# First weight chunks split beside the last output tiles, and a second segment that begins with plain weight blocks

## The reference, cut to what matters

```python
def swiglu_ffn(h, w_in, w_out):
    gate, up = jnp.split(h @ w_in, 2, axis=-1)
    return (jax.nn.silu(gate) * up) @ w_out

for li in range(DEPTH):
    x = x + 0.5 * swiglu_ffn(rmsnorm(x, norms[li, 0]), ffn_w_in[li, 0], ffn_w_out[li, 0])
    h = rmsnorm(x, norms[li, 1])
    ...                                   # conformer_conv (li = 0) or attention (li = 1) gives y
    x = x + y
    x = x + 0.5 * swiglu_ffn(rmsnorm(x, norms[li, 2]), ffn_w_in[li, 1], ffn_w_out[li, 1])
    if li == N_A_LAYERS - 1:
        shared = (rmsnorm(x, norm_kv) @ w_kv).reshape(B, T, N_GROUPS, 2, HEADS_PER_GROUP, HEAD_DIM)
return rmsnorm(x, norm_final), ...
```

## Time and profile before

| | |
|---|---|
| median of 3 runs | 2461.33 us (2458.36 to 2463.57) |
| the profiled execution | 2460.06 us, its span 2458.2 us |
| TensorE busy | 2287.1 us, 93% of the span, 17414 matmuls |
| VectorE busy | 1695.7 us, 69% |
| ScalarE, GpSimd busy | 840.1 us, 34%; 227.4 us, 9% |
| mean granted clock of TensorE | 0.976 |

### The profile page before, as it was taken

How to read it: one execution, slowest core, us unless ns; L and a number is a source line. 1 busy time by engine, 2 the same in 40 slices (tenths; PEclk the granted TensorE clock), 3 DMA queues, 4 the chain that set the end, 5 groups by cost and what they waited for, 6 DMA issues and landing times.

```text
span 2458.2 us, 41111 instructions
## 1 busy us (share of the span) xinstructions
PE 2287.1 (93%) x17414; PEld 2149.9 (87%) x17414; DVE 1695.7 (69%) x2175; ACT 840.1 (34%) x1055; POOL 227.4 (9%) x210
## 2 busy tenths in 40 slices
PE   2999999879889999999998999999999977999998
PEld 1999999877489999998777999999977767999997
DVE  6894796495789947963347974984346569956973
ACT  2442343211344423432223431442145534422431
POOL 3000001201140000011000000003001131000002
PEclk9999999999899999999999999999999988999999
DMA  3353453444334435521347542533759722323321
GB/s 110 115 169 102 128 178 96 128 122 113 76 88 147 154 93 154 160 88 53 114 123 222 171 150 84 167 113 83 205 146 280 219 69 86 92 82 92 94 75 50
DMA packets 372760, 306.61 MB, mean 125 GB/s; under 512 B 13831, under 2 KB 337423, under 8 KB 371723
## 3 DMA queue, kind: packets, MB, share of 16 engines
q1 hardware_dynamic: 367451, 237.47, 34.0%
q0 software_dynamic: 5184, 67.43, 7.9%
HBM read 285.51 MB, written 70.54 MB: 145 GB/s over the span
## 4 chain that ended last, share of the span: by engine, by line
PE 83%; DVE 10%; issue 2%; ACT 2%; SPq 1%; DMA 1%; POOL 0%; POOLq 0%; DVEq 0%
PE ps L1707 29%; PE ps L1764 13%; PE ps L1766 13%; PE ps L1765 13%; PE ps L2017 2%; PE ps L2018 2%; PE ps L2019 2%; PE ps L1899 1%; PE ps L2051 1%; DVE hlS L1248 1%; PE ps L2123 1%; PE ps L2099 1%; PE ps L2134 1%; DVE cT L1466 1%; DVE hlA L1248 1%
## 5 line engine op out<-in xcount | busy, mean ns | idle before, releaser
L942 ACT CAST hlS<-blk 128x1024 fp32r<-128x1024 f32 x176 | 183.3, 1052 | 204.7 <-PE ps L1766 172.6
L1707 PE MATMUL ps<-actH,oWB 128*128 128x288 f32 x1408 | 250.1, 296 | 0.0
L1707 PE MATMUL ps<-actH,oWA 128*128 128x288 f32 x1408 | 249.9, 296 | 0.0
L1764 PE MATMUL ps<-tE,hlS 128*128 128x288 f32 x704 | 212.2, 301 | 15.5 <-DVE hlS L1248 13.1
L1385 DVE SCALAR_TENSOR_TENSOR cs<-ps,rstd 128x576 f32<-128x576 f32 x64 | 48.5, 758 | 257.4 <-PE ps L1707 257.4
L1248 DVE TENSOR_TENSOR hlS<-blk,hlS 128x1024 fp32r<-128x1024 f32 x176 | 217.2, 1238 | 0.0
L1764 PE MATMUL ps<-tM,hlA 128*128 128x288 f32 x704 | 211.4, 300 | 0.0
L1765 PE MATMUL ps<-tE,hlS 128*128 128x288 f32 x704 | 210.3, 299 | 0.0
L1766 PE MATMUL ps<-tE,hlS 128*128 128x288 f32 x704 | 209.9, 298 | 0.0
L1707 PEld LDWEIGHTS ps<-actH,oWA 128*128 128x128 f32 x1408 | 209.2, 189 | 0.7 <-DVE cs L1310 0.2
L1707 PEld LDWEIGHTS ps<-actH,oWB 128*128 128x128 f32 x1408 | 208.8, 189 | 0.0
(11 more groups left out here) (245 smaller groups left out, 5554.6 us busy)
## 6 DMA issues: line engine op xcount, KB each, us to landing
blk<-in_ffn_w_in SPq DMA_DIRECT2D x352, 256.0 KB, 4.0
raws<-in_ffn_w_out SPq DMA_DIRECT2D x64, 704.0 KB, 4.5
out_kv_sample<-in_cache_kv_w POOLq DMA_DIRECT2D x8, 4064.0 KB, 16.2
out_kv_sample<-in_cache_kv_w POOLq DMA_DIRECT2D x8, 2016.0 KB, 8.3
wst<-in_conv_w_pw SPq DMA_DIRECT2D x24, 512.0 KB, 4.2
wst<-in_w_kv SPq DMA_DIRECT2D x24, 512.0 KB, 3.9
kc<-in_cache_kv_w SPq DMA_DIRECT2D x40, 256.0 KB, 8.1
uV<-ucat SPq DMA_DIRECT2D x80, 105.5 KB, 2.2
```

Of the source, the lines that this page charges most:

```text
L942: nc.scalar.copy(o, a).then_inc(S["f_h"], 1)
L1707: nx = nc.tensor.matmul(outs[t], a, b[:, t, :], start=start and first, stop=stop and b is xh and not first)
L1764: nc.tensor.matmul(out, wh[:, cols], TERM[what][:, p, 0], start=p == 0, stop=False)
```

## The change

- Second segments get an order of their own for the first unit's products: P1, P4, P2, P5, P6, P7, P3. TensorE waits for `px` of tile 6 before P1 and for `px` of tile 7 before P2 in place of the blocks of `xT`. ScalarE's waits name all products that use a split.
- VectorE splits SA and SB of that unit before it adds `px` of tile 7 to `xT`, not after.
- The first two chunks of pw1, kv and q are split ahead of tile 6's and tile 7's turn on ScalarE and VectorE, not after tile 7's.
- kv starts chunk by chunk as the blocks of `hH` and `hL` come; the ten small products stand behind chunk 1, the square root and the reciprocals behind the splits of chunks 2 and 3. The first column block is written out of the loop.
- pw1, kv and q wait for `px` of tile 6 before their first product.

```diff
+FIRST = (("P1", "P5", "P6", "P2", "P7", "P4", "P3"), ("P1", "P4", "P2", "P5", "P6", "P7", "P3"))
+def product_table(g):
+    order = [(x, 0) for x in FIRST[g]]
...
# ScalarE: unit_high
-                last = {"A1": "P1", "A2": "P4", "A3": "P4", "SA": "P7", "SB": "P3"}[what]
-                act.wait_ge(S["f_mm"], product_no(n, g, last, u - 1))
+                users = {"A1": ("P1",), "A2": ("P2", "P4"), "A3": ("P1", "P2", "P4"), "SA": ("P6", "P7"),
+                         "SB": ("P5", "P3")}[what]
+                act.wait_ge(S["f_mm"], max(product_no(n, g, x, u - 1) for x in users))
# ScalarE: outputs
                 if g == 1:
+                    if m >= KD - 2 and AFTER[n] != "final":
+                        c = m - (KD - 2)
+                        act.wait_ge(S["f_ready"], split_no(n, 1, "out", KD - 1))
+                        split_high(CB[AFTER[n]] + c, c, SIZE[AFTER[n]])
                     gain_high(AFTER[n], m)
-            if g == 1 and AFTER[n] != "final":
-                for c in range(2):
-                    if c == 0:
-                        act.wait_ge(S["f_ready"], split_no(n, 1, "out", KD - 1))
-                    split_high(CB[AFTER[n]] + c, c, SIZE[AFTER[n]])
# ScalarE: kv
-        std_tokens("kv")
         for n in range(6):
             for s in range(4):
+                if n == 0 and s == 2:
+                    std_tokens("kv")
# VectorE: outputs
+                if g == 1 and m >= KD - 2 and AFTER[n] != "final":
+                    c = m - (KD - 2)
+                    split_low(CB[AFTER[n]] + c, c, SIZE[AFTER[n]])
                 dve.wait_ge(S["fo_mm"], out_no(n, g, m))
...
                 out_low(n, g, m + 2)
+                if g == 0 and m == KD - 1:
+                    units_start(n, 1, ("SA", "SB"))
                 dve.wait_ge(S["px_ready"], out_no(n, g, m))
                 nc.vector.tensor_tensor(xT[:, m], xT[:, m], px[m % 2], ALU.add).then_inc(S["x_ready"], 1)
                 if g == 1:
                     gain_low(AFTER[n], m)
-                elif m >= KD - 2:
-                    units_start(n, 1, ("A1", "A2") if m == KD - 2 else ("SA", "SB"))
-            if g == 1 and AFTER[n] != "final":
-                for c in range(2):
-                    split_low(CB[AFTER[n]] + c, c, SIZE[AFTER[n]])
+                elif m == KD - 2:
+                    units_start(n, 1, ("A1", "A2"))
# VectorE: kv, the reciprocals from ahead of the loop to n == 0, s == 2
...
# TensorE: first unit of a segment
+            else:
+                pe.wait_ge(S["px_ready"], out_no(n, 0, KD - 2))
+                product("P1")
+                ready("A2", 0)
+                product("P4")
+                pe.wait_ge(S["px_ready"], out_no(n, 0, KD - 1))
+                product("P2")
+                ready("SB", 0)
+                product("P5")
+                product("P6")
+                product("P7")
+                product("P3")
# TensorE: kv
-        pe.wait_ge(S["sq_ready"], SQ["kv"])
-        square_sum_tokens()
-        for k in range(KD):
-            pe.wait_ge(S["h_ready"], HB["kv"] + k + 1)
+        pe.wait_ge(S["px_ready"], out_no(1, 1, KD - 2))
+        def kv_columns(n, first):
             for s in range(4):
                 pe.wait_ge(S["w_ready"], n * 4 + (CB["kv"] + s + 1))
+                if first:
+                    pe.wait_ge(S["h_ready"], HB["kv"] + 2 * s + 2)
...
+                if first and s == 1:
+                    pe.wait_ge(S["sq_ready"], SQ["kv"])
+                    square_sum_tokens()
+        kv_columns(0, True)
+        with pe.Fori(1, 6) as n:
+            kv_columns(n, False)
```

More of the change, by code:

```diff
@@ L99, in load_table @@
     return place
-SPLIT, PRODUCT, LOAD = split_table(), product_table(), load_table()
+SPLIT, PRODUCT, LOAD = split_table(), [product_table(g) for g in range(SEGS)], load_table()
 def a_split(u, what):
@@ L113, in product_no @@
 def product_no(n, g, what, u):
-    return (SEGS * n + g) * len(PRODUCT) + PRODUCT[what, u]
+    return (SEGS * n + g) * len(PRODUCT[g]) + PRODUCT[g][what, u]
 def unit_no(n, g, u):
@@ L786, in shift_cache @@
                 if ph in FFN:
-                    pool.wait_ge(S["f_mm"], SEGS * len(PRODUCT) * FFN[ph] + start + at_ * every)
+                    pool.wait_ge(S["f_mm"], SEGS * len(PRODUCT[0]) * FFN[ph] + start + at_ * every)
                 else:
@@ L1526, in _ @@
         feed_forward(1)
[L1529 to L1533, removed]
         for n in range(6):
@@ L1536, in _ @@
                 c = 4 * n + s + 2
+                if n == 0 and s == 2:
+                    dve.wait_ge(S["stdT_ready"], 1)
+                    me.mark(nc.vector.reciprocal(rstdT[:, 0:4], rstdT[:, 0:4]))
+                    nc.vector.reciprocal(rstdT[0:SMP, 4:5], rstdT[0:SMP, 4:5]).then_inc(S["kv_evac"], 5)
+                    me.wait()
+                    dve.wait_ge(S["kv_evac"], 5)
                 if s == 3:
@@ L1731, in body @@
             def body(i, first):
+                if first:
+                    pe.wait_ge(S["px_ready"], out_no(2, 1, KD - 2))
                 for s in range(4):
@@ L1772, in ready @@
                 pe.wait_ge(S["f_ready"], split_no(n, g, what, u))
-            terms = n if g == 0 else None
             ph = f"ffn{n}_in"
-            now = KD * XV[f"ffn{n}" if g else ph]
             ready("A1", 0)
[L1778 to L1787, removed]
-            if g == 0:
+            if g == 0:
+                product("P1", n)
+                pe.wait_ge(S["x_ready"], KD * XV[ph] + KD)
+                if n == 2:
+                    pe.wait_ge(S["kv_evac"], 35)
+                ready("SB", 0)
+                product("P5", n)
+                product("P6", n)
+                product("P2", n)
                 pe.wait_ge(S["sq_ready"], SQ[ph])
                 square_sum().then_inc(S["ss_done"], 1)
-            product("P7", terms)
-            if g == 0:
+                product("P7", n)
                 pe.wait_ge(S["std_ready"], ROUND[ph])
-            product("P4", terms)
-            product("P3", terms)
+                product("P4", n)
+                product("P3", n)
+            else:
[5 more added lines that the diff above has]
+                product("P2")
+                ready("SB", 0)
+                product("P5")
+                product("P6")
+                product("P7")
+                product("P3")
             def cycle(i, u):
@@ L1924, in _ @@
         for c in range(16):
+            if c == 0:
+                pe.wait_ge(S["px_ready"], out_no(0, 1, KD - 2))
             pe.wait_ge(S["w_ready"], CB["pw1"] + c + 1)
@@ L1998, in _ @@
         feed_forward(1)
-        pe.wait_ge(S["sq_ready"], SQ["kv"])
-        square_sum_tokens()
-        for k in range(KD):
-            pe.wait_ge(S["h_ready"], HB["kv"] + k + 1)
+        pe.wait_ge(S["px_ready"], out_no(1, 1, KD - 2))
         hHf, hLf = hH[:].rearrange("p k a b -> p k (a b)"), hL[:].rearrange("p k a b -> p k (a b)")
-        with pe.Fori(0, 6) as n:
+        def kv_columns(n, first):
             for s in range(4):
                 pe.wait_ge(S["w_ready"], n * 4 + (CB["kv"] + s + 1))
+                if first:
+                    pe.wait_ge(S["h_ready"], HB["kv"] + 2 * s + 2)
                 for t in range(TT):
                     r = P if t < 4 else SMP
-                    if s == 0:
+                    if s == 0 and not first:
                         pe.wait_ge(S["kv_evac"], n * 5 + (t + 1))
```

2 lines of the change are left out of this document (removed).

## The result

The changed kernel takes 2424.84 us (median of 4 runs, 2424.05 to 2425.24) against 2461.06 us (2458.36 to 2463.57, 4 runs): ratio 0.9851, 95% interval 0.9837 to 0.9864, 36.2 us saved. The forecast was 2423 with a range of 2416 to 2433.

A forecast was written before the change was run, and what follows sets the result against it. TensorE was taken as busy nearly throughout, with VectorE setting the units' pace (11.22 against 11.10 us). Joins 13.9, pw1 8.4, kv 8.2 and q 7.4 sum to 37.9 us: 2461.3 - 37.9 = 2423.4, said as 2423, range 2416 to 2433.

The forecast's parts named there:

- The joins: First to second segment, four times: VectorE's `up` sum 3.1 us earlier each, plus 1.5 at the third join; 13.9 us in all.
- SB ahead of the x addition: At the joins: the addition to x (0.76 us) behind the splits makes SB ready near 264.7 instead of 265.4.
- The slow stretch of the third join: Third join: TensorE's clock at 0.50 after a 2.4 us gap; no gap, no slow stretch, 1.5 us won.
- that rule's price: Clock-window rule: the third join's 1.5 us are luck and another gap may cost it; sum 36.7 instead of 38.2.
- pw1: Start of pw1: early splits bring the square sum at 464.0 instead of 472.4; 8.4 us, or 0 if loads are late.
- it moves as a whole: In pw1, the chain behind the square sum (square root, reciprocal, split of chunk 2) moves with it, keeping the 8.4 us.
- Rival C: Clock: remaining gaps of 2 to 5 us meet or leave slow stretches, 1.5 to 2.4 us each; 2427 or 2419; chance 0.13.
- rival B: In pw1: the gain is swallowed by waits for SyncE's copies between partitions; 8.4 us lost, 2432; chance 0.10.
- kv: Start of kv: tenth product at 1135.5 instead of 1144.91, less 1.2 us for ten small products; 8.2 us, bounds 7.2 and 8.3.
- q: Start of q, as pw1: square sum at 1722.2 instead of 1729.66; 7.4 us.
- The cover of the splits: Beside tiles 6 and 7: idle engines hide the early pieces, 1.0 and 1.2 us each, to 1.8 beside GpSimd's squares.
- The sum: Whole kernel: 13.9 + 8.4 + 8.2 + 7.4 = 37.9 us saved.

The follow-up runs named there:

- vector_extra: The changed kernel with three tiny dependent VectorE memsets that nobody waits for in units 2 to 11 of every segment: 2444.32 us.
- joins_only: The kernel before with only the four joins changed, the starts of pw1, kv and q as before: 2449.64 us.
- add_first: The changed kernel with the addition to x ahead of the SA and SB splits again at the joins: 2423.61 us.
- warm_fit: The changed kernel with 20 and 17 products that nobody reads in the two longest waits of pw1's convolution: 2421.57 us.
- kv_squares_first: The changed kernel, but TensorE waits for all squares before kv as before; kv's first two chunks still split early: 2435.04 us.
- after_again: The changed kernel once more, unaltered, for a second profile: 2424.21 us.
- starts_only: The changed kernel with the four joins as before, keeping the new starts of pw1, kv and q: 2436.42 us.

## Why the prediction was right, and where it was not

- **The joins** (predicted 4 x 3.1, and 1.5 for the slow stretch; measured 3.16, 3.14, 3.15 and 4.62): right, and for the reason given. Following VectorE's list to its sum for `up` gave 12.5 us, and 12.46 came. vector_extra shows that the list sets the pace, joins_only that the gain is there without the starts. One piece was credited and is worth nothing: SB ahead of the x addition (add_first).
- **The slow stretch of the third join**: the new order takes it away, since no gap is left. By the Trainium skill ("TensorE: Matmul & The Clock Gate", "Part 1: The HAM clock gate") the moment of a change of clock depends on a free-running window. The runs agree so far: the lower clock followed one of four equal gaps in one execution and two of four in another. The prediction sets that rule's price against a sum of 38.2 us (36.7 without the 1.5), but its own sum is 37.9; it should say 36.4.
- **pw1** (predicted 8.4, measured 4.8): the mechanism and its size were right at the square sum, 8.5 us, and the first convolution still begins 8.7 us earlier after the tile (81.38 against 90.05 us). Then the steps behind it shrink the gain. The step that failed is "it moves as a whole". The work moved, but steps behind the waits got longer: the first convolution took 9.62 us where it took 8.56, the last 9.31 where it took 8.92, the selection products behind it (`ps L1969`, `ps L1989` in the chains of work) 3.40 and 1.91. The rows of the two chains, before and after (start, us), and the windows of the selection products:

```profile
547.72 8.56 PE ps L1899 x64
...
635.73 8.92 PE ps L1899 x64
...
653.27 1.91 PE ps L1969 x4
653.30:655.20 1.90, 1.90 (x5) 0.66 (x5) 1.90 (x4) 1.89 (x4) 0.00 (x0) 1.00 0.02 4
```
```profile
536.32 9.62 PE ps L1917 x64
...
625.68 9.31 PE ps L1917 x64
...
643.61 3.40 PE ps L1989 x4
643.60:647.00 3.40, 3.40 (x6) 0.97 (x5) 2.77 (x5) 2.69 (x5) 0.00 (x0) 0.54 0.00 0
```

  That is 1.1 + 0.4 + 1.5 = 3.0 of the missing 3.7 us (8.5 - 4.8); the selection products ran at a clock of 0.54 after and 1.00 before. Rival C named the clock, but in gaps between steps, not inside pw1; rival B named a loss in pw1, but by copies that don't move. warm_fit shows that the clock behind the two waits is worth 6.4 us there. The change isn't what slowed the selection products: they took 3.60 us in joins_only, whose code in pw1 is that of before, and 1.91 in add_first, whose code there is the changed one. So 1.5 of the 3.0 us are luck of the pair of executions. The first convolution took 8.56 and 8.76 us in the two profiles with the code of before and 9.04 to 9.87 in the five with the changed one. Why that part goes with the change is not settled.
- **kv** (predicted 8.2, measured 8.7): right. The small products took 1.15 us, where the sum took 1.2. kv_squares_first lost 10.1, 2.5 of them by slow products; in before the slow stretch behind the same wait was shorter (the earlier trace rows has the 0.23 us from 1144.91 on, 3.8 us after the first).
- **q** (predicted 7.4, measured 9.1): the square sum comes 13.78 us after the tile's `px` before and 6.20 after, 7.6. Another 1.7 us stands in a wait in attention for the key cache, which the sum had not looked at. In TensorE's waits, before and after:

```profile
PE ps L2051 <- DMA kc<-in_cache_kv_w: 2.1, 1, 2.1
```
```profile
PE ps L2077 <- DMA kc<-in_cache_kv_w: 0.4, 1, 0.4
```

  The change didn't shrink this wait: with the changed code in q it was 0.7 us in after_again, 1.0 in starts_only, 2.1 in kv_squares_first and 2.3 in add_first. So the 1.7 us are luck, and the wait alone doesn't set the interval, which was 517.2 us with 0.7 (after_again) and with 2.3 (add_first). In the second profile of after, q's interval saves 7.9 us, close to the prediction.
- **The cover of the splits** was under-priced, 2.44 us each and not 1.2 to 1.8, and it cost nothing: VectorE still waited 2.99 us for TensorE before the last `px`.
- **The sum**, 37.9, was too high by 1.9 us against the 36.0 of the profiled executions: pw1's 3.6 too much met q's 1.7 and kv's 0.5 too little, the joins' 0.2 too little, and 0.7 us more at the start and the end. That it came so close is in part luck: errors of opposite sign.

## What to carry to other kernels

Where two engines are both nearly full, follow a removed gap down both lists to the place after which neither rests: the gain is that of the slower list, here 3.1 us for a gap of 2.4. When TensorE must wait, the wait's price includes the stretch behind it, 2.5 us on 7 in the profile of after; products that nobody reads may buy it back if they end before the wait does, and their duration is to be read from a trace first. A long chain that "moves as a whole" keeps its waits, and the clock behind each of them can come out otherwise in another execution. So a gain that is read from one pair of profiles carries their luck: compare several profiles with the same code in that stretch.

## What the runs showed of the hardware

- After a wait of 2.4 us the granted clock fell to 1.2 GHz (0.50 in the earlier trace rows) in some cases and not in others, at the same place of the same code: 1.5 us each time. After 9.3 and 10.8 us of waiting the convolution was slow in each of the nine profiles without added products in pw1, 8.56 to 9.96 us; with 1.1 to 1.3 us left of those waits it took 7.1 us at a clock of 1.00.
- A product of 128 x 288 whose operands are plain float32 (`rstd`, `ones`) is two instructions and takes 0.49 us at clock 1.00 (19.56 us for 40), against 0.1327 us for one of the reduced type.
- VectorE's subtraction of 128 x 1024 takes 1.22 us alone. It took 2.44 where GpSimd's addition of 128 x 576 had begun before it and ran beside it for 1.4 us. Where VectorE's subtraction had begun first (after, 691.25 us), it kept its 1.22 us and GpSimd's squares took 1.99 us instead of 1.15.
- A chain of three dependent 128 x 2 memsets made VectorE's unit 0.29 us longer (11.49 against 11.20 us), and a join with ten of them 2.51 us longer.
